# Softmax probabilities scaled ahead of their transposes, in the attention loop of a fused decoder layer

## What is computed

```python
def sink_probs(scores, mask, sinks):
    sc = jnp.where(mask, scores, NEG_INF)
    sink = sinks.astype(jnp.float32).reshape(N_KV_HEADS, Q_GROUP, 1, 1)
    m = jnp.maximum(jnp.max(sc, axis=-1, keepdims=True), sink)
    p = jnp.exp(sc - m)
    denom = jnp.sum(p, axis=-1, keepdims=True) + jnp.exp(sink - m)
    return p / denom
...
    p = sink_probs(scores, mask, sinks).astype(vv.dtype)
    o = jnp.einsum("bnkgqs,bnskd->bnqkgd", p, vv).reshape(b, s, ATTN_WIDTH)
```

## Time and profile before

| | us |
|---|---|
| median of 3 runs (966.22 to 970.6) | 968.36 |
| the profiled execution's own time | 970.76 |
| its span, first to last instruction | 968.5 |
| PE busy | 917.4 (95%) |
| DVE busy | 452.8 (47%) |
| ACT busy | 362.7 (37%) |
| POOL busy | 214.6 (22%) |

### The profile page before, as it was taken

How to read it: one execution, slowest core, us unless ns; L and a number is a source line. 1 busy time by engine, 2 the same in 40 slices (tenths; PEclk the granted TensorE clock), 3 DMA queues, 4 the chain that set the end, 5 groups by cost and what they waited for, 6 DMA issues and landing times. The chain is left out here.

```text
span 968.5 us, 16231 instructions
## 1 busy us (share of the span) xinstructions
PE 917.4 (95%) x5401; PEld 825.1 (85%) x5402; DVE 452.8 (47%) x792; ACT 362.7 (37%) x614; POOL 214.6 (22%) x240
## 2 busy tenths in 40 slices
PE   4999998999998999999999999999889999999993
PEld 4777776887998999999999999999877787878872
DVE  4567767342222222232222264444886657576540
ACT  5676654210322111121111142122516657585641
POOL 1434221344220000000000020000132445354451
PEclk9999999999899999999999999999899999999997
DMA  6102021200202101011010045862276989979722
GB/s 218 45 23 81 33 72 34 56 1 5 97 1 75 57 32 65 32 53 45 32 65 32 22 136 206 266 231 79 83 264 238 323 250 302 324 242 321 218 41 39
DMA packets 50927, 114.77 MB, mean 118 GB/s; under 512 B 8205, under 2 KB 26317, under 8 KB 50864
## 3 DMA queue, kind: packets, MB, share of 16 engines
q1 hardware_dynamic: 42352, 96.30, 28.6%
q0 software_dynamic: 7488, 17.85, 7.7%
q10 hardware_dynamic: 1040, 0.00, 0.1%
HBM read 101.57 MB, written 23.00 MB: 129 GB/s over the span
## 5 line engine op out<-in xcount | busy, mean ns | idle before, releaser
L1345 ACT ACTIVATE gate<-psum 128x352 f32<-128x352 f32 x48 | 22.2, 465 | 211.4 <-PE psum L73 211.4
L71 PE MATMUL psum<-w_hi,hT_hi 128*128 128x512 f32 (+3 forms) x216 | 82.1, 380 | 3.8 <-DVE hT_lo L973 3.8
L2109 DVE TENSOR_TENSOR hT_lo<-room,hT_hi (+1 forms) x32 | 72.0, 2287 | 16.0 <-ACT hT_hi L1809 16.0
L71 PE MATMUL psum<-hT_hi,x_xT_hi 128*128 x192 | 77.5, 404 | 1.6 <-DVE x_xT_lo L2285 1.5
L73 PE MATMUL psum<-w_hi,hT_lo 128*128 128x512 f32 (+3 forms) x216 | 78.3, 362 | 0.0
L72 PE MATMUL psum<-w_lo,hT_hi 128*128 128x512 f32 (+3 forms) x216 | 78.2, 362 | 0.0
L71 PE MATMUL psum<-hT_hi,w_hi 128*128 128x352 f32 x240 | 77.4, 323 | 0.0
L72 PE MATMUL psum<-hT_lo,w_hi 128*128 128x352 f32 x240 | 76.9, 321 | 0.0
L73 PE MATMUL psum<-hT_hi,w_lo 128*128 128x352 f32 x240 | 76.9, 320 | 0.0
L73 PE MATMUL psum<-hT_hi,x_xT_lo 128*128 x192 | 75.2, 392 | 0.0
L72 PE MATMUL psum<-hT_lo,x_xT_hi 128*128 x192 | 75.2, 392 | 0.0
(11 more groups left out here) (336 smaller groups left out, 2332.7 us busy)
## 6 DMA issues: line engine op xcount, KB each, us to landing
room<-in_w_gu SPq DMA_DIRECT2D x16, 2048.0 KB, 11.4
dn_raw<-in_w_dn SPq DMA_DIRECT2D x16, 1024.0 KB, 7.0
g_w_raw<-in_w_ab SPq DMA_DIRECT2D x15, 768.0 KB, 4.3
xT_chunk<-in_xT SPq DMA_DIRECT2D x8, 528.0 KB, 3.7
x_in<-in_x SPq DMA_DIRECT2D x8, 512.0 KB, 3.5
out_y<-y SPq DMA_DIRECT2D x8, 512.0 KB, 3.5
hn_rows<-squares SPq DMA_DIRECT2D x8, 512.0 KB, 3.2
o_w_raw<-in_w_out_t SPq DMA_DIRECT2D x7, 512.0 KB, 7.9
```

The costliest lines, as they stand in the source:

```text
L71: eng.matmul(out, lh, rh, start=first and k == 0, stop=False)
L1345: act.activation(gate[:, (ab + c) % 2, :], bank(psum, gate_pair(ab, c))[:, 0:TC], ACT.Sigmoid).then_inc(gated.sem, 1)
L2109: dve.tensor_tensor(gu_lo[:, buf, ks], gu_raw[:, buf, ks], gu_hi[:, buf, ks].bitcast(F32), ALU.subtract).then_inc(gu_lo_made.sem, 1)
```

## The change

The scaling by one over the denominator is made on the probabilities, on DVE, between ACT's exponentials and TensorE's transposes, once for each gp (`scale_p`). There, queries are on the partitions, so the factor is a scalar for each partition. `invert_dens`, `dens_turn`, `copy_rT` and `o_scale` go, with their semaphores. `oa_high` and `oa_low` read PSUM bank 5 itself, and `oa_low(done)` stands at the end of the same step where `oa_low(done-1)` stood in the middle of it. `values` of the next tile, which writes bank 5, waits for `oa_lo_made` in place of `o_scaled`.

```diff
             def probs(t, gp):
...
                 act.wait_ge(s_ready, u + 1)
-                if t >= 1:
-                    act.wait_ge(rd_made, t)
...
             def oa_high(t):
                 if t < PT:
-                    act.wait_ge(o_scaled, t + 1)
-                    src = o_n
+                    act.wait_ge(o_made, 2 * t + 2)
+                    src = bank(psum, 5)
...
             def probs_turn(t, gp):
                 u = 2 * t + gp
-                pe.wait_ge(p_made, u + 1)
+                pe.wait_ge(p_scaled, u + 1)
...
                 if t >= 1:
-                    pe.wait_ge(o_scaled, t)
+                    pe.wait_ge(oa_lo_made, t)
...
+            def scale_p(t, gp):
+
+                u = 2 * t + gp
+                k0 = block_keys(t)
+                dve.wait_ge(p_made, u + 1)
+                step.did(dve.tensor_tensor(rden[:, gp, :], den[:, gp, :], sink_e[:, gp, :], ALU.add))
+                step.did(dve.reciprocal(rden[:, gp, :], rden[:, gp, :]))
+                for kv, i, j, g in heads_of(gp):
+                    ins = dve.tensor_scalar(p_sb[:, gp, j, k0:], p_sb[:, gp, j, k0:], rden[:, gp, j:j + 1], None, ALU.mult)
+                ins.then_inc(p_scaled, 1)
...
                 mask_scores(done, 1)
+                scale_p(done, 0)
                 if s < PT:
                     k_squares(s)
                 if s + 2 < NT:
                     mean_square(s + 2)
                 copy_pT(done, 0)
+                scale_p(done, 1)
                 if s == PT:
                     q_squares(s)
                     k_squares(s)
                 else:
                     k_scale(s)
                 copy_pT(done, 1)
-                if done >= 1:
-                    oa_low(done - 1)
-                invert_dens(done)
...
                 if s == PT:
                     spread_q()
                     vs_low(0)
-                o_scale(done)
-            vs_low(1)
-            vs_low(2)
-            oa_low(PT - 1)
-            vs_low(3)
+                oa_low(done)
+            for c in range(1, 4):
+                vs_low(c)
```

More of the change, by code:

```diff
@@ L161, in attention_phase @@
         s_sb, p_sb = sp_sb[:, 0], sp_sb[:, 1:]
-        rT, o_n = (sp_sb[:, 0, 2 * n:2 * n + 2, :].rearrange("p g c -> p (g c)") for n in range(2))
         z, _ = brief((("z_qkv", [P, AW + KVW]), ("behind_z", [P, G * KV * HD])))
@@ L238, in attention_phase @@
         pT_made, pT_copied = sem("pT_made"), sem("pT_copied")
-        o_made, o_scaled = sem("o_made"), sem("o_scaled")
-        rd_made, rT_made, rT_copied = sem("rd_made"), sem("rT_made"), sem("rT_copied")
+        o_made = sem("o_made")
+        p_scaled = sem("p_scaled")
         oT_made, oa_hi_made, oa_lo_made = sem("oT_made"), sem("oa_hi_made"), sem("oa_lo_made")
@@ L566, in _ @@
                     vs_high(0)
-                    copy_rT(done)
                     vs_high(1)
@@ L581, in _ @@
                     copy_qT(s)
-                    if s > 0:
-                        copy_rT(done)
                     if s + 3 < NT:
@@ L640, in project_q @@
                     pe.wait_ge(z_copied, q_count(t - 1))
-                if t >= 2:
-                    pe.wait_ge(rT_copied, t - 1)
                 mm = product(pe, bank(psum, 0)[0:n, 0:AW], lambda k: (hT[0][:, k0 + k, toks(t)], hT[1][:, k0 + k, toks(t)]),
@@ L714, in values @@
                 mm.then_inc(o_made, 1)
[L716 to L725, removed]
             def sample_scores():
@@ L752, in sample_values @@
                 pe.wait_ge(v_cache_in, DMA)
-                pe.wait_ge(o_scaled, PT)
+                pe.wait_ge(oa_lo_made, PT)
                 for kv in range(KV):
@@ L773, in v_product @@
                     pe.wait_ge(z_copied, 2 * NT)
-                    pe.wait_ge(rT_copied, PT)
                 elif t == 1:
@@ L816, in _ @@
                 qk_turn(s)
-                dens_turn(s - 1)
                 if s + 2 < NT:
@@ L828, in _ @@
             values(PT - 1, 1)
-            dens_turn(PT - 1)
             qk_turn(PT)
@@ L940, in copy_pT @@
                                 psum[:, 6 + first:8, :].rearrange("p a c -> p (a c)")).then_inc(pT_copied, 1)
[L942 to L955, removed]
+            def scale_p(t, gp):
[7 more added lines that the diff above has]
+                ins.then_inc(p_scaled, 1)
             def oa_low(t):
                 dve.wait_ge(oa_hi_made, t + 1)
-                src = o_n if t < PT else bank(psum, 4)
+                src = bank(psum, 5 if t < PT else 4)
                 dve.tensor_tensor(oaT[1][:, :, toks(t)],
```

## The result

The changed kernel takes 988.91 us (median of 5 runs, 987.48 to 989.66), the kernel before 966.68 in 5 runs. The ratio on record is 1.0212, with a 95% interval from 1.0196 to 1.0228; it isn't the quotient of the two medians, which is 1.0230. The forecast was 987.4. As a loss, the forecast was 19.0 us; the medians give 22.2 and the ratio 20.5.

What follows compares the result with a forecast made beforehand. TensorE, busy 95% of the span, was taken as the bound. Steps 2 to 6 +16.9, step 7 +1.5, step 1 +0.6, step 8 0: in all +19.0 us, taking the median from 968.36 to 987.4, range 976 to 996.

Steps and rivals of the forecast that it cites:

- Transposes removed: Four TensorE transposes of `dens_turn` go: 0.43 us in each of steps 1 to 6, about 2.6 in all.
- Price of a scaling: On VectorE, one `scale_p` (add, reciprocal, four multiplications of 0.35 us) takes 1.56 us, upper bound 1.84.
- Wait one: Scores of gp 1: `oa_low(done)` delays the next mask, so TensorE waits 0.80 us in steps 2 to 6.
- Wait two: Transposes of gp 0: `scale_p(done, 0)` follows the mask on VectorE, so they start 1.09 us late.
- Wait three: Transposes of gp 1: `scale_p(done, 1)` runs beside GpSimd's `h_low`, each holding the other; they start 1.91 us late.
- a choice between two readings of the earlier trace: Gp 1's multiplications beside `h_low`: free, ending at 13.31, or held, ending at 14.16; the forecast took held.
- the pace of line 1058: VectorE instruction faster per element than a tensor-tensor, taken to show use of more than one read path.
- Step 1: Loop step on 128 keys, half the width: between 0 and 1.2 us more, taken as +0.6; GpSimd against VectorE nearly tied.
- step 6: One of five full loop steps, 2 to 6, each forecast at 20.28 us, 3.37 more than 16.91.
- rival (d): The clock falls in the loop, once for some 6 us in each of five steps: +15, 1002 us; chance 0.08.
- a granted clock under 1.00 in a step: In the profile after, this in the loop steps would show the forecast wrong.
- The tail: Step 8 loses 1.2 us at its transposes, but PE was idle before `qk_turn`, which starts no later: 0.

Runs made afterwards that it cites:

- run 1: Changed kernel with only `oa_low` put back to its place one step later, ahead of `copy_pT(done, 0)`: 984.32 us.
- run 4: Kernel before the change, with only `oa_low(done)` moved late, to the end of the step behind `o_scale`: 973.47 us.
- Run 3: Changed kernel without the multiplications, add and reciprocal still made: 959.18 us, with fewer expert steps; loop step 17.27 us.
- Runs 2 and 8: Changed kernel with GpSimd's `h_low` made to wait until gp 1 is scaled, 977.51 us; with only its second half waiting, 982.36 us.
- runs 5 to 7: Changed kernel with `oa_low` lagged and `h_low` held, 974.67 us; then gp 1's scores and gp 0's scaling earlier, 971.71; then multiplications shared with ScalarE, 967.09.

## Why the prediction was right, point by point

The mechanism came out as forecast; the closeness of the total is in part luck. The loss was 22.2 us by the medians against a forecast of 19.0. The 987.4 lies only 1.5 below the 988.91 because the kernel before came out at 966.68 in 5 runs, 1.7 below the 968.36 that the forecast started from.

**Transposes removed: right in the full steps, too large for steps 1 and 6.** Between gp 1's transposes and the next step's scores 0.37 came back in each of steps 2 to 5 (5.07 for 5.44). In step 1 it was 0.11 (4.63 for 4.74), and in step 6, read in run 1 where the clock stayed full, 0.11 too (5.07 for 5.18). Both times the scores stood idle 0.25 instead, in step 6 for ScalarE's copy of q. The prediction had counted 0.43 in all six.

**Price of a scaling: right.** 0.35 for a multiplication (348 measured), 1.13 for four (1.14), 1.56 for one `scale_p` (74.53 to 76.07 is 1.54). The working has a slip that changes nothing: with 160 ns as the fixed part, line 1058 pays 0.75 ns an element and not 0.77, and the tensor-tensor 1.02 and not 1.04; both results stay.

**Wait one, the late `oa_low`: right,** 0.80 forecast, 0.75 in the step shown (4.86 for 4.11), 0.74 given back in run 1; run 4 shows it alone in the old kernel.

**Wait two, gp 0's scaling on the path: right,** 1.09 forecast, transposes 1.08 later behind their scores (5.05 against 3.97). Run 3, without the multiplications, has none.

**Wait three, gp 1's scaling beside GpSimd: right, in steps 2 to 5.** 1.91 forecast; 5.19 - 3.39 = 1.80 measured, of which 1.33 is GpSimd's. Runs 2 and 8 show both holds. That the multiplications are held was a choice between two readings of the earlier trace rows, and the runs settle it. The argument for the choice, that the pace of line 1058 tells of a second read path, is not tested by any run.

**Two steps were mis-sized, both downwards.** Step 1, "a near tie" between 0 and 1.2 taken at 0.6, measured 2.3: neither engine simply came first, but two of the four multiplications were held, one through each half of `h_low`, and the transposes waited 2.01. Step 6, 3.4 forecast, measured 5.5: the add was held through both halves, and the clock fell for a stretch. The fall is a small piece of rival (d), once rather than five times, and a granted clock under 1.00 in a step was one of the prediction's own signs of being wrong. Together these made 3.8 us, and the steps between, at 3.0 to 3.3 in place of 3.4, gave back 0.7.

**The tail: right.** The 1.2 us of step 8 vanished in the idle time before `qk_turn`.

What stays open is who goes first at the boundary between two GpSimd instructions while VectorE waits. In steps 2 to 5 the add got in between the halves, in step 6 it didn't, and GpSimd had started 0.58 us ahead of it in step 3 and 0.65 in step 6. The trace of run 1 has the same in each of these steps, so it is not chance from one execution to the next, but no run tells what decides. Nor does one tell what brought the clock down.

## What to carry to other kernels

A scaling on the chain between two TensorE instructions costs its latency, not its work: count from the instruction that releases it to the one that waits, with everything that stands in the same queue, and compare it with the matmuls that lie between. When you add VectorE work, look at what GpSimd does at that very time, also after the work has moved GpSimd; holding GpSimd back by one wait gave back nearly half of the loss here. And move a read of a buffer later or earlier only after asking what is behind it in its queue.

## What the runs showed of the hardware that I had not expected

A VectorE instruction can be held through two GpSimd instructions in a row, 1.87 us for an add of 128x4 that takes 0.15, and which of the two engines goes next differs from step to step, in the same way in two traces. A wait of TensorE of 2.0 to 2.1 us in a busy loop was followed by half clock in two of the four cases in these two traces, at a cost of 1.0 and 1.5 us. And a removed piece of TensorE's work can expose a GpSimd root of 1.64 us that it had covered: the mask started 0.3 us later in runs 5 to 7.
